# The chunked scan of an RWKV-7 mixer: next pair's features at the head of the round, key norm inside the chain

## What is computed

```
def update(s, w_t, k_t, v_t, kk_t, a_t):
    sa = jnp.einsum('ebhvk,ebhk->ebhv', s, kk_t)
    return s * w_t[..., None, :] - sa[..., :, None] * (kk_t * a_t)[..., None, :] + v_t[..., :, None] * k_t[..., None, :]
...
kk = kk / jnp.maximum(jnp.sqrt(jnp.sum(jnp.square(kk), axis=-1, keepdims=True)), 1e-12)
...
yn = ((y - mean) * lax.rsqrt(var + RW_GN_EPS)).reshape(B, L, H * N) * ln_w.astype(f32) + ln_b.astype(f32)
...
return ((yn + bonus).astype(v.dtype) * g) @ w_o
```

## Time and profile before

| | us |
|---|---|
| median of 3 runs | 3305.69 (3305.52 to 3308.08) |
| the profiled execution | 3302.86 |
| its span | 3301.1 |
| PE busy over the span | 2826.6 |
| DVE busy over the span | 944.8 |
| one round of the scan (pair 2) | 79.01 |
| DVE busy in that round | 54.80 |

### The profile page before, as it was taken

How to read it: one execution, slowest core, us unless ns; L and a number is a source line. 1 busy time by engine, 2 the same in 40 slices (tenths; PEclk the granted TensorE clock), 3 DMA queues, 4 the chain that set the end, 5 groups by cost and what they waited for, 6 DMA issues and landing times.

```text
span 3301.1 us, 51847 instructions
## 1 busy us (share of the span) xinstructions
PE 2826.6 (86%) x22761; PEld 1935.9 (59%) x22761; DVE 944.8 (29%) x1486; ACT 586.2 (18%) x864; POOL 539.9 (16%) x539
## 2 busy tenths in 40 slices
PE   6999888588889599999994999477888777699997
PEld 4887443233345499996552554266666673388643
DVE  2000455322330500000007300466677751300001
ACT  3001233211011300000003000322233220301001
POOL 1322000000001133430000000222222210266300
PEclk8999666598889799999997999699999997899998
DMA  5554000100001022111110233221111112132321
GB/s 228 204 216 161 1 0 0 62 0 0 39 0 51 13 64 64 61 63 61 52 36 9 66 89 91 78 36 33 32 34 33 31 19 83 38 93 91 96 77 43
DMA packets 136793, 202.08 MB, mean 61 GB/s; under 512 B 87567, under 2 KB 97359, under 8 KB 129904
## 3 DMA queue, kind: packets, MB, share of 16 engines
q1 hardware_dynamic: 136623, 199.51, 19.1%
HBM read 182.18 MB, written 17.30 MB: 60 GB/s over the span
## 4 chain that ended last, share of the span: by engine, by line
PE 55%; DVE 9%; DMA 3%; POOL 3%; ACT 2%; issue 2%; SPq 2%; ACTq 0%; DVEq 0%; POOLq 0%
PE PS L308 22%; PE PS L285 19%; PE PS L1512 4%; PE PS L866 2%; PE PS L833 1%; POOL scan_back L1453 1%; PE PS L364 1%; POOL scan_back L1452 1%; PE PS L1171 1%; PE PS L857 1%; DVE X L396 1%; DVE PS L377 1%; SPq L1397 1%; SPq L1421 1%; DVE TMP L387 1%
## 5 line engine op out<-in xcount | busy, mean ns | idle before, releaser
L308 PE MATMUL PS<-P,WR 128*128 128x384 f32 (+1 forms) x1312 | 461.4, 515 | 4.2 <-DVE P L341 2.8
L308 PEld LDWEIGHTS PS<-P,WR 128*128 128x128 f32 x1312 | 249.0, 190 | 215.9 <-issue 89.2
L285 PE MATMUL PS<-H_r,TMP_r 128*128 128x384 f32 (+1 forms) x1056 | 320.5, 358 | 24.0 <-DVEq L334 24.0
L285 PE MATMUL PS<-Y_r,TMP_r 128*128 128x384 f32 (+1 forms) x1056 | 320.7, 357 | 16.6 <-DVEq L334 16.6
L265 POOL CAST TMP_r<-WR 128x1024 fp32r<-128x1024 f32 x112 | 116.5, 1040 | 1270.9 <-DMA WR<-in_ffn_w_dram 1050.8
L267 POOL TENSOR_TENSOR WR_r<-WR,TMP_r 128x1024 fp32r<-128x1024 f32 x112 | 267.8, 2391 | 9.0
L285 PEld LDWEIGHTS PS<-H_r,TMP_r 128*128 128x128 f32 x1056 | 195.5, 189 | 40.3 <-issue 24.6
L285 PEld LDWEIGHTS PS<-Y_r,TMP_r 128*128 128x128 f32 x1056 | 194.7, 189 | 32.6 <-issue 17.4
L377 DVE RECIPROCAL PS<-TMP 128x768 f32<-128x768 f32 (+1 forms) x8 | 34.9, 4361 | 610.7 <-ACT TMP L356 610.7
L341 DVE TENSOR_TENSOR P<-TMP,PS 128x768 f32 (+1 forms) x44 | 36.1, 821 | 584.7 <-PE PS L285 584.7
L285 PE MATMUL PS<-H_r,WR_r 128*128 128x384 f32 x704 | 182.4, 340 | 0.0
(11 more groups left out here) (253 smaller groups left out, 4126.9 us busy)
## 6 DMA issues: line engine op xcount, KB each, us to landing
WR<-in_ffn_w_dram SPq DMA_DIRECT2D x88, 512.0 KB, 3.5
TMP<-in_mod_w_dram SPq DMA_DIRECT2D x40, 1024.0 KB, 5.4
WR<-in_ffn_w_dram SPq DMA_DIRECT2D x32, 704.0 KB, 4.0
WR<-in_mix_w_in_dram SPq DMA_DIRECT2D x24, 512.0 KB, 6.1
WR<-in_rw_w_rkv_dram SPq DMA_DIRECT2D x24, 512.0 KB, 4.2
P<-in_mod_w_dram SPq DMA_DIRECT2D x4, 2048.0 KB, 21.1
vkr_dram<-P SPq DMA_DIRECT2D x16, 384.0 KB, 4.8
scan_front<-vkr_dram SPq DMA_DIRECT2D x16, 384.0 KB, 3.2
```

What stands on the lines that cost most here:

```text
L285: last = nc.tensor.matmul(PS[:, 2 * s + b, 0:h1 - h0], w, x[:, h0:h1], start=k + p == 0, stop=k == CT - 1 and p == 2)
L308: last = nc.tensor.matmul(PS[:, bank + b, 0:h1 - h0], WR[:, s, k, :], d.rhs(k0 + k)[:, h0:h1], start=begins and k == 0, stop=ends and k == ...
```

## The change

Six moves, no instruction added or taken away in the scan but one extra turn of the loop (i runs to 8, so that pair 7 can be finished).

1. DVE: `sums keys removed` of pair n for direction 0 and `sums` for direction 1 stand ahead of pair i's first masks; `keys removed` of direction 1 and `mA_0` ahead of its first subtractions; `mA_1` right behind them. `added` comes later.
2. DVE: the finish of pair i (`rec f1 f2 z`) moves into the next round, in two pieces around `w32`.
3. DVE, ACT, PE: the key norm of pair c moves from the end of the round into the chain, `kk` behind step 5, `kmax krec kmul` between steps 6 and 7.
4. PE: all four `lora` first, `A_0` behind `w16`, `A_1` behind `y16_1`; the token transposes shift by one place.
5. ACT: `kc ksq kroot` ahead of the token copies.
6. SP: the block copies ahead of the keys' loads.

```diff
--- before.py
+++ after.py
-                for it in range(-2, CT):
+                for it in range(-2, CT + 1):
...
         PEM = Marks(pe_done, (
-            (1, "l00 l01"), (0, "w16_0 w16_1"), (1, "l10 l11"), (0, "x16_0 y16_0 x16_1 y16_1 w32_0 w32_1 y32_0 y32_1"),
-            (1, "A_0"), (0, "ok_0 obv_0 ok_1 obv_1 m_0 m_1"), (1, "A_1"), (0, "n_0 n_1 r yt"),
+            (1, "l00 l01 l10 l11"), (0, "w16_0 w16_1"), (1, "A_0"), (0, "x16_0 y16_0 x16_1 y16_1"), (1, "A_1"),
+            (0, "w32_0 w32_1 y32_0 y32_1 ok_0 obv_0 ok_1 obv_1 m_0 m_1 n_0 n_1 r yt"),
             (0, "c0_1 c1_1 cg c0_2 c1_2"), (1, "K_0"), (0, "c0_3 c1_3"), (1, "CD_0"), (0, "c0_4 c1_4"), (1, "K_1"),
-            (0, "c0_5 c1_5"), (1, "CD_1"), (0, "c0_6 c1_6"), (1, "tV"), (0, "c0_7 c1_7"), (1, "tB_0"),
-            (0, "c0_8 c1_8"), (1, "tK_0"), (0, "c0_9 c1_9"), (1, "tB_1"), (0, "c0_10 c1_10"), (1, "tK_1"),
-            (0, "ys"), (1, "kT_0"), (2, "kk"), (1, "kT_1"), (0, "mean"), (1, "BV_0 BV_1"), (0, "var")))
+            (0, "c0_5 c1_5"), (2, "kk"), (1, "CD_1"), (0, "c0_6 c1_6"), (1, "tV"), (0, "c0_7 c1_7"), (1, "tB_0 tK_0"),
+            (0, "c0_8 c1_8"), (1, "tB_1"), (0, "c0_9 c1_9"), (1, "tK_1"), (0, "c0_10 c1_10"), (1, "kT_0"),
+            (0, "ys"), (1, "kT_1"), (0, "mean"), (1, "BV_0 BV_1"), (0, "var")))
         DV = Marks(dve_done, (
-            (0, "w16_0 w16_1"), (1, "scan_0"), (0, "x16_0 y16_0 x16_1 y16_1"),
-            (1, "kin_0 first_0 ends_0 rt_0 rate_0"), (0, "w32_0 w32_1"), (1, "ba_0 bt_0 scan_1"), (0, "y32_0 y32_1"),
-            (1, "kd_0 acc_0 kt_0 mA_0 kin_1 first_1 ends_1 rt_1 rate_1 ba_1 bt_1"), (0, "m_0 m_1"), (1, "mA_1"),
-            (0, "n_0 n_1 r"), (1, "kd_1 acc_1 kt_1 accr"),
+            (1, "scan_0 kin_0 first_0 ends_0 rt_0 rate_0 ba_0 bt_0 scan_1"), (0, "w16_0 w16_1"),
+            (1, "kin_1 first_1 ends_1 rt_1 rate_1 ba_1 bt_1 mA_0"), (0, "x16_0 y16_0 x16_1 y16_1"), (1, "mA_1"),
+            (-1, "rec f1"), (0, "w32_0 w32_1"), (-1, "f2 z"), (0, "y32_0 y32_1"), (1, "kd_0 acc_0 kt_0"),
+            (0, "m_0 m_1"), (1, "kd_1 acc_1 kt_1 accr"), (0, "n_0 n_1 r"),
             (0, "st0_1 st1_1 bonus st0_2 st1_2"), (1, "mK_0"), (0, "st0_3 st1_3"), (1, "mCD_0"), (0, "st0_4 st1_4"),
-            (1, "mK_1"), (0, "st0_5 st1_5"), (1, "mCD_1"), (0, "st0_6 st1_6 st0_7 st1_7 st0_8 st1_8 st0_9 st1_9"),
-            (0, "st0_10 st1_10 ysum cen"), (2, "kmax krec kmul"), (0, "rec f1 f2 z")))
+            (1, "mK_1"), (0, "st0_5 st1_5"), (1, "mCD_1"), (0, "st0_6 st1_6"), (2, "kmax krec kmul"),
+            (0, "st0_7 st1_7 st0_8 st1_8 st0_9 st1_9 st0_10 st1_10 ysum cen")))
         AC = Marks(act_done, (
-            (1, "t00 t01 ep_0 en_0 t10 t11 ep_1 en_1"), (0, "ok_0 obv_0 ok_1 obv_1 yt gt"),
-            (1, "tV tB_0 tK_0 tB_1 tK_1"), (2, "kc ksq"), (1, "kT_0"), (2, "kroot"), (1, "kT_1"), (0, "sq"),
-            (1, "bv_0 bv_1"), (0, "groot")))
+            (1, "t00 t01 ep_0 en_0 t10 t11 ep_1 en_1"), (0, "ok_0 obv_0 ok_1 obv_1 yt gt"), (2, "kc ksq kroot"),
+            (1, "tV tB_0 tK_0 tB_1 tK_1 kT_0 kT_1"), (0, "sq"), (1, "bv_0 bv_1"), (0, "groot")))
         PO = Marks(pool_done, ((1, "s00 s01 s10 s11 zero sub turn"),))
...
                         sp.wait_ge(pe_done, PEM["l11", n])
                     sp.dma_start(W2S, w2[c]).then_inc(lora2_in, 16)
                     sp.dma_start(A2S, a2[c]).then_inc(lora2_in, 16)
-                    if c:
-                        sp.wait_ge(dve_done, DV["accr", n])
-                    sp.dma_start(KDIR, vkr_dram[1, c]).then_inc(keys_in, 16)
-                    sp.dma_start(RDIR, vkr_dram[2, c, :, 0:L]).then_inc(keys_in, 16)
                 if here(n):
...
                     sp.dma_start(BLK.rearrange("q (e n) -> q e n", e=2),
                                  blk_dram.rearrange("e x p b s t -> (x p b) e (s t)")).then_inc(blk_back, 16)
                 if here(c):
+                    if c:
+                        sp.wait_ge(dve_done, DV["accr", n])
+                    sp.dma_start(KDIR, vkr_dram[1, c]).then_inc(keys_in, 16)
+                    sp.dma_start(RDIR, vkr_dram[2, c, :, 0:L]).then_inc(keys_in, 16)
                     if c:
                         sp.wait_ge(pe_done, PEM["tV", n])
...
                 if here(n):
-                    lora(n, 0, 0)
-                    lora(n, 0, 1)
+                    for e in range(2):
+                        lora(n, e, 0)
...
                     chain(i, 5)
+                if here(c):
+                    b = front("kk", c)
+                    pe.wait_ge(act_done, AC["ksq", c])
+                    for h in range(2):
+                        last = nc.tensor.matmul(PS[:, b + h, 0:HALF], HONES, KS[:, HALF * h:HALF * h + HALF],
+                                                start=True, stop=True)
+                    PEM.done(last, "kk", c)
                 if here(n):
...
+            def finish(i):
+                v.wait_ge(act_done, AC["groot", i])
+                DV.done(nc.vector.reciprocal(FIN, FIN), "rec", i)
+                after("rec", i)
+                DV.done(nc.vector.scalar_tensor_tensor(YS, YS, pcol(PLW, i), FIN, ALU.mult, ALU.mult), "f1", i)
+
+            def gated(i):
+                after("f1", i)
+                DV.done(nc.vector.scalar_tensor_tensor(YS, YS, pcol(PLB, i), EB, ALU.add, ALU.add), "f2", i)
+                after("f2", i)
+                DV.done(nc.vector.tensor_tensor(Z[:, i, :], YS, GTS, ALU.mult), "z", i)
+
...
+                if here(n):
+                    sums(n, 0)
+                    keys(n, 0)
+                    removed(n, 0)
+                    sums(n, 1)
                 if here(i):
                     level(i, 0, 0)
                     level(i, 0, 1)
                 if here(n):
-                    sums(n, 0)
+                    keys(n, 1)
+                    removed(n, 1)
+                    mask_gram(n, 0, "A_0", "mA_0", AM[:, n % 2, 0])
                 if here(i):
                     for e in range(2):
                         lessen(i, f"x16_{e}", XY[:, e])
                         lessen(i, f"y16_{e}", XY[:, 2 + e])
                 if here(n):
-                    keys(n, 0)
+                    mask_gram(n, 1, "A_1", "mA_1", AM[:, n % 2, 1])
+                if here(i - 1):
+                    finish(i - 1)
                 if here(i):
                     level(i, 1, 0)
                     level(i, 1, 1)
-                if here(n):
-                    removed(n, 0)
-                    sums(n, 1)
+                if here(i - 1):
+                    gated(i - 1)
                 if here(i):
```

More of the change, by code:

```diff
@@ L1346, in strided @@
             return bass.AP(ap.tensor, ap.offset, [list(ap.ap[0])] + [list(d) for d in dims])
-        ROUNDS = [(it, it + 1, it + 2) for it in range(-2, CT)]
+        ROUNDS = [(it, it + 1, it + 2) for it in range(-2, CT + 1)]
         def here(n):
@@ L1556, in scan_pe @@
                 if here(n):
-                    lora(n, 0, 0)
-                    lora(n, 0, 1)
+                    for e in range(2):
+                        lora(n, e, 0)
+                        lora(n, e, 1)
                 if here(i):
@@ L1568, in scan_pe @@
                 if here(n):
-                    lora(n, 1, 0)
-                    lora(n, 1, 1)
+                    pe.wait_ge(dve_done, DV["bt_0", n])
+                    gram(n, "A_0", 0, AA[0], KIN[0])
                 if here(i):
@@ L1577, in scan_pe @@
                         PEM.done(squares(b, Wm(e), Ym(e)), f"y16_{e}", i)
+                if here(n):
+                    pe.wait_ge(dve_done, DV["bt_1", n])
+                    gram(n, "A_1", 1, AA[1], KIN[1])
+                if here(i):
                     for e in range(2):
@@ L1679, in scan_pe @@
                     tokens(n, "tB_0", AA[0])
+                    tokens(n, "tK_0", SU[0])
                 if here(i):
@@ L1682, in scan_pe @@
                 if here(n):
-                    tokens(n, "tK_0", SU[0])
+                    tokens(n, "tB_1", AA[1])
                 if here(i):
@@ L1686, in scan_pe @@
                 if here(n):
-                    tokens(n, "tB_1", AA[1])
+                    tokens(n, "tK_1", SU[1])
                 if here(i):
@@ L1701, in scan_pe @@
                     PEM.done(last, "ys", i)
-                if here(n):
-                    tokens(n, "kT_0", KIN[0])
-                if here(c):
-                    b = front("kk", c)
-                    pe.wait_ge(act_done, AC["ksq", c])
-                    for h in range(2):
-                        last = nc.tensor.matmul(PS[:, b + h, 0:HALF], HONES, KS[:, HALF * h:HALF * h + HALF],
-                                                start=True, stop=True)
-                    PEM.done(last, "kk", c)
                 if here(n):
@@ L1763, in scan_act @@
                     AC.done(nc.scalar.activation(GTS, PS[:, front_bank("cg", i) + 1, 0:L], ACT.Copy), "gt", i)
-                if here(n):
-                    tokens(n, "tV", VTT)
```

(34 more changed lines are left out.)

14 lines of the change are left out of this document (2 added, 12 removed).

## The result

The changed kernel takes **3358.56 us** (median of 4 runs, 3357.47 to 3365.57) against 3305.61 of the kernel before on the same chip: **1.0163 times**, 95% interval 1.0146 to 1.0181, slower by 53 us. Forecast were 3352 us and 0.91 for slower.

A forecast was written before the change was run, and what follows sets the result against it. It took a loop of waits through the inverses, no engine full, as the bound. Terms of 32.6 us plus 13.8 for the clock gave +46.4: 3349 on the profiled execution, 3352 us as median; range 3322 to 3374.

The forecast's parts named there:

- first loop: Present bound of a round: inverses land, `w16` to `accr`, SP, POOL's inversion, SP, inverses land; PE idled 6.4 us.
- the second one: Loop of V, next pair's features, masks, products, chain, next V; said to set the round once the inverses don't.
- V: The end of `var`, PE's last piece of a round; 9.2 us ahead of the next pair's `w16` before.
- The head: V to end of `obv_1`: 40.0 us against 37.6, so +2.4; features in 9.6 us, as pair 0 took, POOL's halvings included.
- one clock term: One spell of about 4 us at half PE clock on the path per round: +2.3 us, between 0 and 5.
- `obv_1` to V: Rest of the round: +5.0 us, mainly 6.5 of key norm between steps 6 and 7, less 2.0 after `ys`.
- rival (c): PE's own pauses in `n` and `yt` shrink, 4 us a round come back: 3324 us, chance 0.08.
- The sum: Pairs 1 to 5 +37.0, pair 6 +1.6, pairs 7 and 0 about -3 each, clock 13.8: +46.4 us.
- (d): Rival: features fit DVE's gap and the chain hides the key norm, so faster: 3261 us, chance 0.04.
- (a): Rival: the clock costs nothing more than before, as slow `w16` leaves the path: 3338 us, chance 0.2.
- (b): Rival: clock low through the whole head, eight products about 1.1 us slower each: 3372 to 3385 us, chance 0.12.
- (e): Rival: SP's wait for `tV` keeps the inverses last; time of (a) or more, no chance of its own given.

The follow-up runs named there:

- a_sp_old: The changed kernel with SP's part taken back, so the loads of keys and receptance stand ahead of the block copies again: 3365.89 us, ratio 1.0183.
- a_fill: The changed kernel with eight products that nobody reads added per round on PE, beside `krec`: 3344.84 us, ratio 1.0107.
- a_knorm_end: The changed kernel with the key norm put back to the end of the round: 3310.76 us, ratio 1.0005.
- b_sp: The kernel before with SP's block copies ahead of the keys' loads and nothing else changed: 3259.57 us, ratio 0.9854.

## Why the prediction was right, step by step

- **"The change frees the first loop. What counts is then how long the second one is": right.** No wait for the inverses is left, and a_sp_old sends the blocks 23 us later in the rounds without lengthening them (V of pair 0 to V of pair 7: 581.5 us, 584.4 after; the five full rounds 89.5 each, 88.8 after).
- **The head, 40.0 after V: 42.9 measured.** The first sums at 3.9 and the order of all pieces were as walked. The masks ended 0.6 later: the first sums took 2.37 us beside POOL and 1.75 in pair 0's row, so they were not "in the 9.6 us of pair 0 already", though the other two slow pieces were. `mA_1` ended 2.0 later (28.0), mostly because `x16_1 y16_1` ran slow; the end of `obv_1` was 0.9 more, with `y32`'s products slow too. Of this the prediction had only its one clock term. And 37.6 joined the gap of the next round to this round's 28.4; pair 2's own round had 38.8 before. Over five rounds this stretch grew by 5.1 us, where +2.4 stood, half of what it cost.
- **`obv_1` to V, +5.0: measured 45.8 against 41.5, +4.4, with 2.2 of clock in it** (+5.5 over five rounds). Key norm +6.1 and after `ys` -1.9, as priced; between steps 1 and 6, where `kk` now stands, +1.3. The stretch from `obv_1` to step 1 is 3.0 shorter, not 0.8: besides `A_1`, one pause of PE ("issue") is 0.4 instead of 1.3, and `yt`, which ran slow before (clock 0.56 in 2351 to 2353), runs at full clock. That is a small piece of rival (c); the other two pauses are there still (1.8 and 2.2, with 1.8 and 1.7 before).
- **"If one such spell ... comes to stand on the path ... I take +2.3": right in place and near in size for the chain (2.0 a round, a_fill).** But the head had its own share, which the 2.3 did not cover. The Trainium skill (TensorE: Matmul & The Clock Gate, "HAM oscillation") would let each burst behind a wait start cold. The traces agree in part: three bursts of pair 2's round did, but in a_knorm_end `y32` ran at full speed behind the same wait in this round and slow (4.3 to 5.4 us) in others:

```profile
2330.38 3.02 PE L1511 MATMUL PS<-scan_back 64*64 64x64 f32 x96 [3.43 <-DVE scan_back L1812]
```

- **The sum.** Five full rounds 52.7 against 37.0 + 11.5; pair 6 +5.0 against 1.6 + 2.3; pair 7 -2.6 against -3. Pair 0 was +1.7 against -3, a mis-sized term: its masks came 4.3 earlier (2150.3, 2154.6 before), 2.45 of that because the scan began earlier, but masks to V took 6.0 longer, as it too has the late features and a key norm in its chain. 46.4 became 56.8 in the profile and 53 in the medians: inside the range. That it came so near is in part luck: per round the first stretch was 2.7 us above its term, and the second with the clock's 2.3 in it 1.8 below (5.5 against 7.3).
- **The rivals.** (d), 3261, fell where it was said to be decided: features alone miss the gap. b_sp shows that SP's part, with all else left in place, comes to 3260. (a) fell by the clock's 2.0 us a round in the chain. (b) was right that the head has slow spells too, but the head came out 2.9 us above the walk, not the 8.8 of its eight products. (e) did not happen.

The cause is settled by adding parts in turn: before 3307, + SP's part 3260 (-48), + features and masks at the head, with PE's order 3308 (+48), + late finish 3311 (+3, within the spread), + key norm in the chain 3359 (+48).

## What to carry to other kernels

Freeing the loop that comes last gains only the distance to the next one, so count the idle engine's work in that gap before putting more there: a reciprocal of 5 us belongs where its engine has slack (beside PE's long products), not between two steps that wait for each other. Price each part of a many-part reorder alone and in company: here one move on SP's queue was worth 48 us, two of the DVE moves cost 48 each, and the same key norm cost nothing, 31 or 48 us by what else had been done. If PE must idle under another engine's long instruction, products that nobody reads can keep its clock up: they paid beside the 4.85 us wait of the chain, and six more at each of two shorter waits did not.
